# A two-network kernel on one core: a state-space stage that is summed and scanned in PSUM, sparse heads with compressed scores on the same weights, and three changed orders at stage borders

## The reference

```python
# S5: a complex diagonal recurrence in 64 groups of 64 states, then GELU and a gate
bu = einsum(u, bb)                       # complex drive, every step and state
x[t] = ab * x[t-1] + bu[t]               # complex, scanned over time
y = gelu(Re(x @ c) + d * u)
return y * sigmoid(y @ w_glu)

# sparse mixer: 16 heads; three softmax branches with gates
o_cmp = softmax(q @ k_cmp.T * scale + bias) @ v_cmp     # 15 compressed blocks
o_slc = softmax(q @ k_slc.T * scale + bias) @ v_slc     # 256 keys, causal
o_win = softmax(q @ k_win.T * scale + bias) @ v_win     # 256 keys, causal
o = g0 * o_cmp + g1 * o_slc + g2 * o_win
return o @ w_o
```

## Time and profile before

| | |
|---|---|
| median of 3 runs | 1796.44 us |
| lowest, highest | 1790.84, 1808.46 us |
| the profiled execution | 1802.36 us, its span 1800.5 us |
| PE busy | 1776.0 us, 99% of the span |
| DVE, ACT, POOL busy | 66%, 48%, 32% |
| mean granted PE clock | 0.996 of full |

### The profile page before, as it was taken

One profiled execution on the slowest core, in us unless ns is written; L12 is line 12 of the kernel. 1 busy time (PEld: TensorE's weight loads), 2 busy tenths in 40 slices (PEclk: granted clock), 3 DMA queues, 4 the chain that ended last, 5 costly groups with the idle time before them and its releaser, 6 DMA issues.

```text
span 1800.5 us, 35650 instructions
## 1 busy us (share of the span) xinstructions
PE 1776.0 (99%) x15466; PEld 1723.4 (96%) x15470; DVE 1185.1 (66%) x1372; ACT 872.7 (48%) x1110; POOL 583.7 (32%) x719
## 2 busy tenths in 40 slices
PE   9999999999999999999999999999999999999999
PEld 7999999999999999999999789999999999789999
DVE  7877666766665676676665866555765556856554
ACT  6454445544344544464444344334664446864442
POOL 5977880386664587400000520000000002520000
PEclk9999999999999999999999999999999999999999
DMA  7556656454454466658555425565456653016552
GB/s 265 181 211 227 225 215 207 167 182 170 165 173 155 163 222 225 215 183 345 193 188 195 176 99 206 209 221 211 167 182 220 203 201 134 25 48 211 191 200 102
DMA packets 53799, 336.59 MB, mean 187 GB/s; under 512 B 7899, under 2 KB 11020, under 8 KB 16908
## 3 DMA queue, kind: packets, MB, share of 16 engines
q1 hardware_dynamic: 46272, 300.00, 46.8%
q10 hardware_dynamic: 3276, 19.64, 3.0%
q0 software_dynamic: 4096, 14.68, 2.3%
HBM read 318.54 MB, written 15.75 MB: 186 GB/s over the span
## 4 chain that ended last, share of the span: by engine, by line
PE 87%; DVE 5%; POOL 4%; ACT 1%; issue 1%; DMA 1%; SPq 0%; ACTq 0%; POOLq 0%; DVEq 0%
PE psum L492 27%; PE psum L494 26%; PE psum L493 26%; DVE w_lo L2059 2%; POOL swap L1976 1%; DMA raw<-in_weights 1%; ACT w_hi L1236 1%; PE psum L614 1%; PE psum L844 1%; PE psum L1129 1%; POOL con L2019 1%; PE psum L1146 1%; PE psum L867 1%; POOL con L2011 0%; PE psum L1163 0%
## 5 line engine op out<-in xcount | busy, mean ns | idle before, releaser
L492 PE MATMUL psum<-both,w_hi 128*128 128x256 f32 x3584 | 1006.4, 281 | 9.0 <-DVE both L2066 4.1
L494 PE MATMUL psum<-both,w_lo 128*128 128x256 f32 x3584 | 995.4, 278 | 0.0
L493 PE MATMUL psum<-both,w_hi 128*128 128x256 f32 x3584 | 995.4, 278 | 0.0
L2059 DVE TENSOR_TENSOR w_lo<-raw,w_hi 128x2048 fp32r<-128x2048 f32 x276 | 653.2, 2369 | 253.0 <-ACT w_hi L1236 252.3
L1236 ACT ACTIVATE w_hi<-raw 128x2048 fp32r<-128x2048 f32 (+1 forms) x282 | 536.2, 1903 | 540.8 <-PE psum L494 525.8
L492 PEld LDWEIGHTS psum<-both,w_hi 128*128 128x128 f32 x3584 | 674.8, 188 | 21.8 <-issue 12.2
L494 PEld LDWEIGHTS psum<-both,w_lo 128*128 128x128 f32 x3584 | 676.4, 189 | 0.0
L493 PEld LDWEIGHTS psum<-both,w_hi 128*128 128x128 f32 x3584 | 675.3, 188 | 0.5 <-issue 0.2
L1822 POOL TENSOR_TENSOR rs_tok<-var_tok,nhalf 128x2 f32<-128x2 f32 x11 | 7.8, 710 | 815.5 <-DVE var_tok L2093 815.5
L492 PE MATMUL psum<-hid_hi,w_hi 128*128 128x256 f32 x640 | 178.5, 279 | 0.0
L493 PE MATMUL psum<-hid_lo,w_hi 128*128 128x256 f32 x640 | 177.3, 277 | 0.0
(11 more groups left out here) (406 smaller groups left out, 2000.1 us busy)
## 6 DMA issues: line engine op xcount, KB each, us to landing
raw<-in_weights SPq DMA_DIRECT2D x279, 1024.0 KB, 4.9
table<-tables ACTq DMA_DIRECT2D x8, 1792.0 KB, 9.5
tables<-st POOLq DMA_DIRECT2D x16, 512.0 KB, 5.4
tables<-st POOLq DMA_DIRECT2D x8, 256.0 KB, 6.3
tables<-turns POOLq DMA_DIRECT2D x8, 256.0 KB, 4.4
w<-in_cmp_w ACTq DMA_DIRECT2D x4, 512.0 KB, 5.5
tbl<-in_cmp_w ACTq DMA_DIRECT2D x4, 512.0 KB, 5.4
tbl<-bias_v SPq DMA_DIRECT2D x128, 16.0 KB, 4.7
```

Of the source, the lines that this page charges most:

```text
L492: nc.tensor.matmul(out, a_hi, b_hi, start=start, stop=False, skip_group_check=True)
L493: nc.tensor.matmul(out, a_hi, b_lo, start=False, stop=False, skip_group_check=True)
L494: return nc.tensor.matmul(out, a_lo, b_hi, start=False, stop=stop, skip_group_check=True)
L2059: tt(w_lo[:, g % RING], raw[:, g % RING], w_hi[:, g % RING].bitcast(F32), ALU.subtract).then_inc(sem["lo_ready"], 1)
```

## The change

- The turned drive is multiplied and added in place in its PSUM bank, and scanned from there. One chunk of `states` waits for the scan instead of the turn. PE runs four chunks ahead, and the inner products of two chunks are interleaved, with outputs on the two halves of the partitions (`inner`).
- DVE turns back chunk 3 as well as chunk 7; POOL the other six. `u2` is filled by pairs of chunks (`MOVES`), with the first inputs made earlier; DVE makes inputs 6 and 7 after the first scan. The warm-up matmuls go from 18 to 11, four others go away.
- Tables 5, 6, 7 come in two parts each (`load_outer`, `load_rest`), the first part as soon as the slot's outer part is free.
- In the heads the 15 compressed keys lie ahead of the selected keys, so the compressed scores come out of the same two matmuls. Compressed probabilities of both token blocks are turned by one transpose (padded to 32), with padded, zeroed values (`vcmp`, made by 8 matmuls instead of 4), so their product takes 4 matmuls of 128 columns instead of 2 of 256.
- All three branches are scaled by POOL in three operations; `n_high` moves from ACT to DVE, into `n_low`.
- Orders: in the last convolution triple the scaling comes ahead of the taps; in `ple` of layer 0 `split(g + 3)` moves behind `x_low(r, 3)`, and the next norm ahead of `split(g + 4)`; in `glu` ACT splits ahead of `residual` for the first three units.

```diff
 def states(c):
     if c >= 4:
-        pe.wait_ge(sem["drive"], c - 3)
+        pe.wait_ge(sem["z_ready"], 2 * (c - 3))
...
-    for jj in range(JJ):
-        nc.tensor.matmul(y_of(c, jj), u2[:, jj, c, :], t_[:, jj],
-                         start=False, stop=False, skip_group_check=True)
+def inner(c):
+    pair = (c, c + 1)
...
+    for jj in range(JJ):
+        for d in pair:
+            nc.tensor.matmul(y_of(d, jj), u2[:, jj, d, :], t_[d - c][:, jj], ...)
...
-for c in range(3):
+for c in range(4):
     states(c)
-keep_warm(4, XB)
+    if c % 2:
+        inner(c - 1)
 for c in range(KC):
     outputs(c)
-    if c + 3 < KC:
-        states(c + 3)
+    if c + 4 < KC:
+        states(c + 4)
+        if c % 2:
+            inner(c + 3)
```

```diff
 # DVE, state-space stage
-tt(m1[c % 2][:], s_, e[:, 0:1].broadcast_to([P, 2, SEQ]), ALU.mult)
-tt(m2[c % 2][:, 0], s_[:, 1], e[:, 1], ALU.mult)
-tt(m2[c % 2][:, 1], s_[:, 0], e[:, 2], ALU.mult)
-tt(a_[:], a_[:], b_[:], ALU.add)
-dve.tensor_tensor_scan(z5[c % 2][:, ri], decay, a_[:, ri], 0.0, ...)
+tt(m2[c % 2][:, 0], s_[:, 1], e[:, 1], ALU.mult)
+tt(m2[c % 2][:, 1], s_[:, 0], e[:, 2], ALU.mult)
+tt(s_, s_, e[:, 0:1].broadcast_to([P, 2, SEQ]), ALU.mult)
+tt(s_, s_, m2[c % 2][:], ALU.add)
+dve.tensor_tensor_scan(z5[c % 2][:, ri], decay, two(SB_[c % 4])[:, ri], 0.0, ...)
...
+for c in range(KC):
+    turn(c)
+    scan(c)
+    if c == 0:
+        for d in range(6, KC):
+            inputs(d)
+    if c - 1 in ON_DVE:        # ON_DVE = (3, KC - 1)
+        turn_back(c - 1)
+turn_back(KC - 1)
```

```diff
 # ACT, state-space stage
-move(0)
-move(1)
+for pair in range(3):
+    move(pair)
+act.wait_ge(sem["bu_done"], 3)
+load_outer(5)
+load_outer(6)
+move(3)
...
 for b in range(3):
     act.wait_ge(sem["y_done"], b + 1)
-    load_table(TSLOTS + b)
+    load_rest(5 + b)
     if b == 1:
+        load_outer(7)
         gelu(0)
```

```diff
 # PE, heads
-for br in range(2):
-    nc.tensor.matmul(bank[:, 0:P], q[:, 0:P], ks[rows, br, a, 0:P], ...)
-    nc.tensor.matmul(bank[:, P:P + SEQ], q[:, P:SEQ], ks[rows, br, a, :], ...)
-for t in range(TT):
-    nc.tensor.matmul(DB[0][:, 3 * P + t * NCMP:...], q[:, t * P:(t + 1) * P], kcmp[rows, a, :], ...)
+nc.tensor.matmul(DB[0][:, 0:Q1], q[:, 0:P], ks[0][rows, a, 0:Q1], ...)        # 15 + 128 columns
+nc.tensor.matmul(DB[0][:, Q1:FAR.stop], q[:, P:SEQ], ks[0][rows, a, :], ...)  # 15 + 256 columns
+nc.tensor.matmul(DB[1][:, NEAR], q[:, 0:P], ks[1][rows, a, 0:P], ...)
+nc.tensor.matmul(DB[1][:, FAR], q[:, P:SEQ], ks[1][rows, a, :], ...)
```

```diff
 # POOL, heads
-for t in range(TT):
-    pool.tensor_scalar(lgc[:, b, t], lgc[:, b, t], fac[:, b, 0, t:t + 1], None, ALU.mult)
-pool.tensor_scalar(lg_of[b][:, 1, 0:P], ...)
-pool.tensor_scalar(lg_of[b][:, 1, P:3 * P], ...)
+own = lgc[:, b, :, 0:NCMP]
+tt(own, own, fac[:, b, 0, :].unsqueeze(2).broadcast_to([P, TT, NCMP]), ALU.mult)
+for t, cols in enumerate((slice(0, P), slice(P, 3 * P))):
+    both_ = lg_of[b][:, :, cols]
+    tt(both_, both_, fac[:, b, 1:3, t:t + 1].broadcast_to([P, 2, cols.stop - cols.start]), ALU.mult)
```

```diff
 # borders: DVE in ple, ACT in glu
-split(g + 3)
+if l:
+    split(g + 3)
 scaled(3)
...
 x_low(r, 3)
+if l == 0:
+    split(g + 3)
+    norm(r)
 split(g + 4)
...
 act_fn(tb[:], two(DB[m % 2]), ACT.Sigmoid)
+if m < PAIRS - 1:
+    split(BASE["glu"] + m)
 residual(R_GLU, m)
-split(BASE["glu"] + m)
```

More of the change, by code:

```diff
@@ L384, in program, with landed @@
         sem = {name: ctx.enter_context(nc.semaphore(name)) for name in SEM_NAMES}
-        table_landed = [ctx.enter_context(nc.semaphore(f"table_landed{i}")) for i in range(TSLOTS)]
+        tables_landed = {name: ctx.enter_context(nc.semaphore(f"tables_{name}"))
+                         for name in ("first", "fifth", "outer", "rest5", "rest6", "rest7")}
+        OUTER = {5: ("outer", 32), 6: ("outer", 32), 7: ("rest6", 32)}
+        REST = {5: ("rest5", 16), 6: ("rest6", 32), 7: ("rest7", 16)}
+        def landed(c, part):
+            name, count = ("first", 64) if c < TSLOTS - 1 else ("fifth", 16) if c < TSLOTS else part[c]
+            return tables_landed[name], count
         stored = [ctx.enter_context(nc.semaphore(f"stored{i}")) for i in range(2)]
@@ L1056, in values_out @@
                 pe.wait_ge(sem["k_scaled"], 3)
[L1057 to L1061, removed]
+                for t in range(TT):
+                    for kh in range(KVH):
+                        a, half = kh // 2, kh % 2
+                        last = nc.tensor.matmul(XB[32 * t:32 * t + NCMP, 256 + kh * HD:256 + (kh + 1) * HD],
+                                                hg[:, half, a, 0:NCMP], w2[:, 1, :],
+                                                start=True, stop=True, skip_group_check=True)
                 last.then_inc(sem["w2_done"], 1)
@@ L1157, in n_values @@
                 pe.wait_ge(sem["n_ta"], heads[1] + 1)
-                for b in range(2):
-                    nc.tensor.matmul(out[b], vcmp[:, 2 * (ch // 4) + b, :], ptc[:, b, :], start=True, stop=False,
-                                     skip_group_check=True)
+                for t in range(TT):
+                    for b in range(2):
+                        nc.tensor.matmul(out[b][:, t * P:(t + 1) * P], vcmp[:, t, 2 * (ch // 4) + b, :], ptc[:, b, :],
+                                         start=t == 0, stop=False, skip_group_check=True)
                 for br in range(2):
@@ L1598, in _, with move @@
             norm(R_FFN0)
[L1600 to L1604, removed]
-                    last = copy(u2[32 * i:32 * i + 32, q, 4 * half:4 * half + 4, :], u5_of(q, half)[:, :, i, :])
+            def move(pair):
+                act.wait_ge(sem["u5_ready"], 2 * pair + 2)
+                for to, of in moves("act", pair):
+                    last = copy(to, of)
                 last.then_inc(sem["u2_act"], 1)
@@ L1696, in copy_values @@
                 act.wait_ge(sem["w2_done"], 2)
-                copy(vcmp[:].rearrange("c k d -> c (k d)"), XB[0:NCMP, 256:512]).then_inc(sem["vc_ready"], 1)
+                for t in range(TT):
+                    own = slice(32 * t, 32 * t + NCMP)
+                    last = copy(vcmp[own, t].rearrange("c k d -> c (k d)"), XB[own, 256:512])
+                last.then_inc(sem["vc_ready"], 1)
                 act.dma_start(wg[:], A["gate_w"]).then_inc(sem["wg_landed"], 16)
@@ L1774, in _ @@
                     n_exp(step)
-                if step >= 4 and step % 2 == 0:
-                    n_high((step - 4) // 2)
                 if step == 3:
@@ L1997, in _ @@
             pool.wait_ge(sem["fill_done"], 9)
-            for half in range(2):
-                pool.wait_ge(sem["u5_ready"], 4 * half + 4)
-                for q in range(JJ):
-                    last = pool.tensor_copy(u2[3 * 32:4 * 32, q, 4 * half:4 * half + 4, :], u5_of(q, half)[:, :, 3, :])
+            for pair in range(len(MOVES["pool"])):
+                pool.wait_ge(sem["u5_ready"], 2 * pair + 2)
+                for to, of in moves("pool", pair):
+                    last = pool.tensor_copy(to, of)
                 last.then_inc(sem["u2_pool"], 1)
-            pool.wait_ge(sem["u2_pool"], 2)
-            for c in range(KC - 1):
+            pool.wait_ge(sem["u2_pool"], len(MOVES["pool"]))
+            for c in range(KC):
+                if c in ON_DVE:
+                    continue
+                turned = pool_turns(c)
                 e = table[c % TSLOTS][:, T_E:T_D].rearrange("p (e j k) -> p e j k", e=3, j=JJ)
@@ L2392, in conv_triple @@
                     split(g0 + 1, k)
+                if last:
+                    done(g0 + 2, k)
+                    tt(tc[:], two(XB), rs_b, ALU.mult).then_inc(sem["b_scaled"], 1)
                 for tap in range(1, 3):
```

198 lines of the change are left out of this document (112 added, 86 removed).

## The result

The changed kernel takes 1783.1 us (median of 12 runs, 1779.7 to 1789.0), the kernel before 1799.4 us (12 runs, 1790.8 to 1811.0): a ratio of 0.990, 95% interval 0.987 to 0.992. In two later comparisons on other chips the ratio was 0.992 (0.989 to 0.995) and 0.989 (0.986 to 0.992). The forecast was 1784 and -12.6 us. The medians differ by 16.3 us, and the three ratios stand for -14 to -20 us, some -18. About 13 of these lie in the stretches that the forecast named, though not each in the size that it gave; the rest doesn't.

What follows compares the result with a forecast made beforehand. PE, busy 99% of the span, was taken to bound the kernel, with DVE and POOL also near their limits in the state-space stage. Terms -5.5 - 5.2 + 0.4 - 1.0 - 1.4 + 0.1 = -12.6 us gave 1783.9, range 1772 to 1792.

Steps and rivals of the forecast that it cites:

- State-space stage: From `ffn0` to `glu`: earlier DVE start and faster chunks on DVE and POOL give -5.5 us.
- The rival of contention that stays: State-space stage: PSUM forms cost more or tables arrive late; stage gains 1 to 3 us, total 1787 to 1789; chance 0.22.
- the turned-back chunk: State-space stage: turning back chunk 3 costs DVE 3.2 us, with only its first operation contended.
- POOL's price: State-space stage: 256-element products take 0.61 us where DVE reads PSUM, so a POOL chunk takes 3.95 us, not 4.96.
- the estimate from the page: State-space stage: a PSUM source costs 65 ns more per affected DVE instruction, 2 us over the stage; left out of the sum.
- Heads: Sparse heads: fewer matmuls, one transpose fewer and less DVE work, across DVE's and PE's regimes, give -5.2 us.
- `vcmp`: Compressed values ahead of the heads: four further matmuls cost +0.4 us, bounds 0 and 1.
- `glu`: Border of `glu`: splitting first on ACT removes the 1.57 us wait, -1.4 us, bounds 0 and -1.6.
- `ple`: Border of `ple`: moving the split brings `x_low(3)` 1.3 us earlier and the rope chain about 1.0; -1.0 us.
- Convolution: Last convolution triple: scaling ahead of the taps gives +0.1 us, the 1.8 us wait stays; bounds -0.7 and +0.7.
- rival b: Convolution and heads: two or three clock falls are spared too, with full relief -18 to -22 us, 1775 to 1779; chance 0.16.
- Rival c: State-space stage: PE's clock falls in new gaps and stays down, +10 us, 1806; chance 0.04.

Runs made afterwards that it cites:

- the run in SBUF: Changed kernel with the state-space sums and scans back in SBUF tiles, all else kept: ratio 0.994 (0.991 to 0.997) to the kernel before.
- the scaling on DVE: Changed kernel with the selected branch scaled by two DVE operations a head as before: ratio 0.992, heads 107.5 us with 17.1 us at the low clock.
- the heads alone: Kernel before with only the sparse heads' part of the change: ratio 0.994 (0.992 to 0.997), heads 101.47 us.
- the scores apart: Changed kernel with the compressed scores made by two matmuls of 15 columns of their own, as before: ratio 0.995 (0.992 to 0.997), heads 105.4 us.
- the fillers: Zero matmuls filling PE's gaps in the changed kernel's state-space stage: ratio 0.988 with all gaps filled, 0.989 with two filled and chunk 3 on POOL.
- the last experiment: Changed kernel with two gaps filled, chunk 3 turned back by POOL and one zero matmul more in `ffn1`: ratio 0.989 (0.986 to 0.992).

## Why the prediction was right, and where it was short

- **State-space stage**, -5.5 forecast, -5.1 to -5.3 measured at the full clock. DVE starts 11.8 us behind `ffn0`'s last residual in place of 13.6, 1.8 earlier (forecast 1.9). The chunk is 3.51 us on DVE (3.6) and 3.92 on POOL (3.95). The rival of contention that stays is excluded by the scans at 1.26 us beside POOL. What was mis-sized is the turned-back chunk: 4.0 us, not 3.2 (the terms listed for it add up to 2.84). All four of its operations read two SBUF operands, and I let the first alone contend; in the trace it was the other three, 1.49, 0.94 and 1.11 us in place of 0.41, 0.41 and 0.69. I had it as a gain of the change; it is a loss of 1.8. Inputs 6 and 7, on SBUF too, took 2.2 us beside POOL where the forecast had 1.5. Both slips are hidden in the total, since eight chunks at 3.51 in place of 3.6 give 0.7 back.
- **POOL's price.** The forecast took 0.61 us for a product "where DVE reads PSUM" from the earlier trace rows. That row doesn't show it: DVE stood idle for 0.98 us up to 82.35 and then worked on the SBUF tiles `vp` and `yc`. Beside DVE on PSUM the products take 0.73, 0.4 less than before and not 0.5. The chunk came out at 3.92 against 3.95 because POOL's closing addition fell too, from 1.38 to 1.18 us, which the forecast did not count: the 3.95 was met by luck. Two rows of the kernel before, then one of the changed kernel:

```profile
82.35 2.85 DVE L2398 SCALAR_TENSOR_TENSOR yc<-vp,vec,yc 128x256 f32<-128x256 f32 x4 [0.98 <-ACT yc L1474]
...
1020.31 1.38 POOL L2019 TENSOR_TENSOR con<-con,n 128x512 f32<-128x512 f32 x1
```
```profile
1015.61 1.18 POOL L2073 TENSOR_TENSOR con<-con,n 128x512 f32<-128x512 f32 x1
```

- **Where DVE reads.** The SBUF contention that the Trainium skill states (GPSIMD Engine Reference, section Specifications) is what the run in SBUF shows, 2.07 against 1.28 us for the scans. The higher fixed cost of a PSUM source in the Trainium skill (VectorE: DVE Perf Modes, section on the TRN2 errata) isn't seen: additions of 512 elements take 0.70 us in PSUM and, with POOL waiting, 0.69 in SBUF, the pair of scans 1.26 and 1.28. By busy time it costs at most 0.01 us an operation, and from the start of an addition to the start of its scans 0.83 in place of 0.80; the estimate from the page was 0.065. The measurement decides.
- **Heads**, -5.2 forecast, -6.4 to -7.1 measured at equal low clock. The scores gave 0.31 us a head (0.30), but 4.2 in all: the forecast counted them for ten heads, 3.0, and gave the other six to DVE alone. `n_values`' four matmuls in place of two cost nothing (0.58 us and 0.59; the forecast had +0.5). What the scaling on DVE was worth stays open, 0.6 to 2.7 us by its run, where I had 1.7 for all of DVE's relief. The transpose that went away, 0.11 us a head, was counted for nine heads; no run tests it alone. The pair came to 8.36 us where I wrote 8.5, so the term that was too small is the one for the regime in which PE is the limit.
- **`vcmp`**: +0.4 forecast; the stretch from the norm behind the keys to the norm of the heads went from 225.9 to 226.1 us, +0.2, in every kernel with the heads' part.
- **`glu`**: -1.4 forecast, -1.4 to -1.6 measured, and the wait of 1.57 us is gone.
- **`ple`**: -1.0 forecast, -0.3 to -0.5 measured (from its norm to the end of attention 284.9 us in three profiles with the old order and 284.7 in the first, 284.4 to 284.6 with the new). The step that failed is "I find `x_low(3)` 1.3 us earlier". It is 0.7 earlier, counted from the residual ahead of the moved split: with the split out of the way DVE waits 1.04 us for PE's unit. PE's wait for `x_low(3)` is 1.10 us where it was 1.58 and I expected 0.3 to 0.6. Of the 0.7 us 0.3 is left when the rope chain begins with the cosines, since the later split now stands between `diag` and the cosines (DVE in order of time, with PE's wait at 328.18):

```profile
323.03 0.69 DVE L2344 TENSOR_TENSOR ta<-psum,rs 128x512 f32<-128x512 f32 x1 [1.04 <-PE psum L529]
...
328.18 0.38 PE L527 MATMUL psum<-both,w_hi 128*128 128x256 f32 x1 [1.10 <-DVE both L2122]
...
333.03 2.29 DVE L2115 TENSOR_TENSOR w_lo<-raw,w_hi 128x2048 fp32r<-128x2048 f32 x1
335.23 0.42 DVE L2487 TENSOR_TENSOR cos_rs<-rope_c,rs 128x256 f32<-128x256 f32 x1
```

- **Convolution**: +0.1 forecast, +0.35 measured up to the norm of `ple` (279.8 us against 280.15, profiles without low clock), within the bound of one scaling. It is no scatter: three profiles with the old order have 279.8, seven with the new 280.15 to 280.20, and one 280.6. The wait there isn't one number, though, and it goes by PE's pace. The row of 228 matmuls ahead of it took 118.1 ns a matmul in eight profiles and 113.7 in six (with the heads alone, then the changed kernel, columns as in rows 2):

```profile
59.50:86.40 26.90, 26.87 (x228) 26.90 (x228) 22.35 (x21) 10.61 (x12) 25.81 (x28) 1.00 0.52 196
```
```profile
60.60:86.40 25.80, 25.80 (x227) 25.80 (x228) 22.30 (x21) 9.98 (x10) 24.79 (x27) 1.00 0.58 205
```

Where it ran at the fast pace PE came 1.0 us earlier and waited 1.8 us in either order; where it ran at the slow one it waited 0.74 in the old order and 1.7 in the new. All 14 profiles fit that.

Together, convolution and `ple` took 564.7 us up to the end of attention with the old orders (without low clock) and 564.6 to 564.8 with the new, 565.0 once: the two orders gave nothing, where the forecast had -0.9.
- **The clock** (rival b) came in half, on the mean and not in the profile: 4.7 us of the 18. The two profiles have the same 6.8 us in the heads; only the means over runs show the term. Added to the -13.3 of the terms above it gives -18, between the -14 and the -20 us of the comparisons. That the forecast's 1784 met 1783 is in part luck: the median it started from, 1796.4 of three runs, rose to 1799.4 with twelve, and the clock, which the sum had at nothing, made up for that.
- **Rival c**, a clock that falls in the new gaps, happens too: 6.8, 3.4, 3.4 and 17.1 us low in the stage, in four profiles of the change. All are below the 25 us that it needed to decide. They cost 2.7 us at 6.8, 3.7 at 17.1 and nothing or 1.6 at 3.4, mostly less than the half us per us of the forecast, which fits the slack that PE has there, as it can catch up in what were its waits. The stage of before had such a fall too, once in four, 3.4 us for 1.6.

Open: why fewer falls meet the new heads (the scores apart bring the loss back to 11.8 us, the scaling hardly does, with errors of 1.5 to 1.9), and whether the fillers really hold the clock.

## What to carry to other kernels

Where DVE and POOL both work on SBUF, price DVE's operations by operand place: here one operand in PSUM took both engines out of each other's way, and the rows of a trace tell it if the same form occurs beside POOL and alone. An engine's share that is to be relieved is priced at the new rates, not at the old: the same change that made POOL fast enough made DVE's help a loss. Divide two profiles at the same instructions before crediting a change with their difference: here 9 of 21 us were the state of two executions, and only means over many runs showed what the clock gives.

## What the runs showed of the hardware

- **Two paces of PE.** A long row of 128x128x256 matmuls with a weight load each, at full clock and without waits, runs at 113.3 or 117.8 ns a matmul and keeps it: 1463 in a row, 6.5 us of difference. The shorter row in the convolution has two paces as well, 113.7 and 118.1 ns, and not together with `ffn1`: the changed kernel's second profile had both slow, its first both fast, and the kernel before, in its first profile, the fast one there and the slow one in `ffn1`. In `ffn1` it was 113.3 in 5 and 117.8 in 9 of 14 profiles; in three of one and the same kernel, the changed one, 113.3, 117.8 and 113.3. In `ffn0`, `ffn2` and `ffn3` it was 113.3 each time. The first matmuls of the row stand in the two profiles at the same distances, to 0.01 us. The one matmul more ahead of it, in the last experiment, didn't prevent the slower pace. What decides it stays open.
- **The clock's falls move.** They stand at places that differ between executions of one kernel: the convolution's, of the earlier trace rows, came in 3 of 14 profiles, for 6.8 or 3.4 us, each time behind a wait of 1.81 us and a row at the fast pace; but the changed kernel's first profile passed the same 1.81 us at full clock. A fall's price moves too: in the heads 17.1 us more at the low clock cost 5.9 us in one pair of profiles, 3.4 us more cost 1.6 in another.
